# Preparing the first unit of gated linear attention inside the input projection

## The chip, the cores and the metric

One Trainium2 core runs one program. The time is device microseconds of one execution; smaller is better. Before the change three timed executions gave 2419.51, 2427.17 and 2428.51 us (median 2427.17).

## The reference, cut to what matters

Two transformer blocks run one after the other on 1024 tokens of width 1024. The part that the change touches is the first block's input projection and its gated linear attention (GLA):

```python
z = n @ w_in[i]
gq, gk, gv, g_low, g_r, c_q, c_kv, k_r = split_cols(z, IN_SPLITS)
...
log_a = jax.nn.log_sigmoid((g_low @ gla_gate_w2[i] + gla_gate_b[i]).astype(jnp.float32)) / GLA_TAU
...
b = jnp.cumsum(gi, axis=2)
o_inter = jnp.einsum('bhtk,bhkv->bhtv', qi * jnp.exp(b), state)
scores = jnp.einsum('bhtk,bhsk,bhtsk->bhts', qi, ki, decay)
...
o_g = rms_norm(o_g, gla_out_norm[i]).reshape(B, S, GLA_WIDTH) * jax.nn.silu(g_r)
```

The scores need query and key multiplied by decays that are made from the running sum `b` of the log gates. The second block's modulation, `silu(cond) @ ada_w + b`, is also computed inside the GLA program.

## The kernel before, in words

The kernel is a row of programs, each an `nc.Block()` with a hand-written instruction order for each engine and a barrier behind it. Two of them matter here.

**`project_and_prepare`** (tiles `pp_*`) multiplies the normed input by `w_in`, group of columns by group, and at the same time prepares the queries and keys of the softmax attention (MLA). Its time runs in steps `s`: each step is one projection slot on TensorE (24 matmuls of 256 columns in the last 32 slots), and from step 5 on each token tile `t` of 128 tokens takes a period of 7 steps (`piece(s)`), in which TensorE makes the up-projections (`queries_up`, `keys_up`) and, for the tile before, four groups of transposes `turn(t-1, m)`. Each turned group goes through one PSUM bank (`turn_bank`): ScalarE copies it out (`high`, L614), VectorE takes the remainder (`low`, L784), and only then may TensorE turn the next. ScalarE also takes each projected result out of its bank (`take`, L573; two banks, so the slot two further on waits for it), and VectorE normalises (`normed`) and rotates (`rope`) the heads. SyncE stores the results with DMAs, the last of them behind the last `low`.

**`gated_linear_attention`** (tiles `gla_*`) works on 4 units (token half by pair of heads) of 4 chunks each. A unit needs a preparation, `prep(u, 0..3)`: TensorE multiplies the gates (`gates`, L1386, a float32 matmul), ScalarE makes the logarithm (L1140 to L1143), VectorE the running sum (L1262) and the differences for each level (L1240), ScalarE the exponentials (L1154 to L1173), VectorE the five decayed queries `qs` (L1251) and GpSimd the five decayed keys `ks` (L1104). The preparation of unit u+1 is spread over the chunks of unit u. That of unit 0 has no cover: nothing can be scored before it (`scores(0)`, L1398 and L1405). After the scores of the next chunk come `outputs(n)` and, after every even chunk up to 10, `modulate` (L1460): 8 matmuls over two pieces `ada_w` of 1 MB that stream from HBM through 4 buffers. SyncE issues all loads in the order of its program.

## Time and profile before

| | |
|---|---|
| profiled execution, time | 2428.71 us |
| its span on the core | 2426.9 us |
| median of three timed executions | 2427.17 us |
| TensorE busy in the span | 2274.8 us (94%) |
| input projection, until the GLA program's first instruction | 0 to 273.7 us |
| GLA program | 273.7 to about 394 us |

The profile comes from one execution. Its time lies 1.8 us above its span, and 1.5 us above the median of the timed ones. A row of the timeline gives start, duration, engine, line, operation and, in brackets, how long the engine sat idle before it and what ended that. A releaser is inferred from semaphore events.

### The profile page before, as it was taken

To read this page: it belongs to the slowest core of one execution; us is meant where nothing else is said; L and a number is where in the kernel's file an instruction comes from. 1 tells how busy PE (TensorE), PEld (TensorE's weight loads), DVE (VectorE), ACT (ScalarE), POOL (GpSimd) and SP (SyncE) were. 2 spreads that over 40 slices of the span, in tenths; PEclk is the share of its full clock that TensorE was granted. 3 is DMA by queue.
4 is the path that set the end of the run, shared out by engine and by line. 5 is a ranking of instruction groups with operands and counts; after the bars stand their busy time and mean duration, and the time that the engine had idled before them with its cause. 6 is when DMAs were issued, how large, how long until landed. Compare 5 with 4: busy or idle time off the path is not lost. (4 is left out here: it accounts for less than half of the span.)

```text
span 2426.9 us, 31960 instructions
## 1 busy us (share of the span) xinstructions
PE 2274.8 (94%) x12292; PEld 1889.2 (78%) x12292; DVE 1126.7 (46%) x1992; ACT 976.5 (40%) x1993; POOL 861.4 (35%) x755
## 2 busy tenths in 40 slices
PE   6999487979999999999999999999999899999798
PEld 6799346967888888888887887888888688888566
DVE  4555486861522222222223535044421788888435
ACT  5434344861523113112113426233221677677422
POOL 5433153543323123123123216332210577777331
PEclk9999688999999999999999999999999899999999
DMA  5455745522111112012012112366656335533231
GB/s 149 104 159 132 226 166 166 135 67 74 46 54 57 33 50 70 25 50 66 29 46 65 57 35 66 113 177 204 188 149 179 100 92 128 142 96 96 100 126 78
DMA packets 202281, 248.48 MB, mean 102 GB/s; under 512 B 63592, under 2 KB 123384, under 8 KB 202128
## 3 DMA queue, kind: packets, MB, share of 16 engines
q1 hardware_dynamic: 196368, 240.14, 34.5%
q10 hardware_dynamic: 5760, 6.29, 0.8%
q8 instruction: 97, 1.59, 0.3%
q14 instruction: 56, 0.46, 0.1%
HBM read 172.88 MB, written 65.10 MB: 98 GB/s over the span
## 5 line engine op out<-in xcount | busy, mean ns | idle before, releaser
L2088 POOL TENSOR_TENSOR rm_w_lo<-rm_stage,rm_w_hi 128x512 fp32r<-128x512 f32 x192 | 246.8, 1298 | 653.8 <-ACT rm_w_hi L2158 653.2
L2158 ACT ACTIVATE rm_w_hi<-rm_stage 128x512 fp32r<-128x512 f32 x192 | 118.2, 628 | 287.8 <-PE rm_down L242 234.4
L2795 DVE TENSOR_REDUCE da_low_score<-da_scores 128x1 f32<-128x1280 f32 x128 | 190.3, 1488 | 31.2 <-PE da_scores L2675 31.1
L242 PE MATMUL rm_down<-rm_w_hi,rm_h_hi 128*128 128x512 f32 x512 | 203.7, 398 | 0.0
L242 PE MATMUL rm_down<-rm_w_lo,rm_h_hi 128*128 128x512 f32 x512 | 203.0, 396 | 0.0
L242 PE MATMUL rm_down<-rm_w_hi,rm_h_lo 128*128 128x512 f32 x512 | 202.9, 396 | 0.0
L2346 DVE TENSOR_TENSOR residual<-residual,rm_down 128x512 f32<-128x512 f32 x128 | 87.5, 687 | 225.8 <-PE rm_down L242 225.1
L2778 POOL TENSOR_TENSOR da_prob<-da_prob 128x1280 f32<-128x1280 f32 x64 | 188.2, 2941 | 5.3
L2736 ACT ACTIVATE da_prob<-da_scores,da_low_score 128x1280 f32<-128x1280 f32 x128 | 170.7, 1334 | 7.3 <-DVE da_low_score L2795 7.3
L2675 PE MATMUL da_scores<-da_k_hi,da_q 128*128 128x512 f32 (+1 forms) x384 | 151.7, 395 | 20.3 <-ACT da_prob L2736 9.2
L2337 DVE TENSOR_TENSOR rm_act_r<-rm_act_r 128x512 f32<-128x512 f32 x64 | 45.5, 711 | 222.2 <-ACT rm_act_r L2201 222.2
L2776 POOL TENSOR_SCALAR da_prob<-da_prob,da_ratio 128x1280 f32<-128x1280 f32 x64 | 86.0, 1343 | 173.4 <-DVE da_ratio L2803 173.2
L2675 PE MATMUL da_scores<-da_k_lo,da_q 128*128 128x512 f32 (+1 forms) x384 | 133.7, 364 | 0.0
L2745 ACT ACTIVATE da_aT_hi<-da_turn 128x512 fp32r<-128x512 f32 (+1 forms) x192 | 94.8, 532 | 62.9 <-PE da_turn L2689 62.7
L2810 DVE TENSOR_TENSOR da_aT_lo<-da_turn,da_aT_hi 128x512 fp32r<-128x512 f32 (+1 forms) x192 | 109.1, 596 | 22.1 <-ACT da_aT_hi L2745 20.3
L2201 ACT ACTIVATE rm_act_r<-rm_up 128x512 f32<-128x512 f32 x64 | 38.5, 601 | 194.0 <-PE rm_up L242 193.9
L242 PEld LDWEIGHTS rm_down<-rm_w_hi,rm_h_lo 128*128 128x128 f32 x512 | 96.5, 189 | 23.5
L242 PEld LDWEIGHTS rm_down<-rm_w_lo,rm_h_hi 128*128 128x128 f32 x512 | 96.6, 189 | 23.1
L242 PEld LDWEIGHTS rm_down<-rm_w_hi,rm_h_hi 128*128 128x128 f32 x512 | 96.6, 189 | 23.0
L242 PE MATMUL rm_up<-xa_hi,rm_w_hi 128*128 128x512 f32 x288 | 113.1, 393 | 0.7 <-POOL xb_lo L2116 0.7
L242 PE MATMUL rm_up<-xa_lo,rm_w_hi 128*128 128x512 f32 x288 | 112.7, 391 | 0.0
L242 PE MATMUL rm_up<-xb_hi,rm_w_hi 128*128 128x512 f32 x288 | 112.1, 389 | 0.5 <-POOL rm_w_lo L2088 0.5
(395 smaller groups left out, 6216.4 us busy)
## 6 DMA issues: line engine op xcount, KB each, us to landing
rm_stage<-in_w_mlp_up SPq DMA_DIRECT2D x64, 256.0 KB, 2.8
rm_stage<-in_w_mlp_down SPq DMA_DIRECT2D x64, 256.0 KB, 2.9
rm_stage<-in_da_w_in SPq DMA_DIRECT2D x64, 256.0 KB, 3.3
gla_ada_w<-in_ada_w SPq DMA_DIRECT2D x12, 1024.0 KB, 6.9
da_k_hi<-dk_hi SPq DMA_DIRECT2D x32, 320.0 KB, 7.5
da_k_lo<-dk_lo SPq DMA_DIRECT2D x32, 320.0 KB, 9.1
dp_swapped<-dp_x SPq DMA_DIRECT2D x128, 64.0 KB, 2.0
da_q<-dq SPq DMA_DIRECT2D x32, 256.0 KB, 6.1
```

The costliest lines, as they stand in the source:

```text
L242: last = nc.tensor.matmul(out, x, y, start=(n == 0), stop=(n == total - 1))
L2088: nc.gpsimd.tensor_tensor(lo, stage[:, n % SLOTS], hi.bitcast(F32), ALU.subtract).then_inc(w_lo_ready, 1)
L2158: nc.scalar.activation(hi, stage[:, n % SLOTS], ACT.Copy).then_inc(w_hi_ready, 1)
L2337: nc.vector.tensor_tensor(act_r[:, n % 2], act_r[:, n % 2], act_r[:, n % 2], ALU.mult)\
L2346: nc.vector.tensor_tensor(c.H[:, t, cols_of(half)], c.H[:, t, cols_of(half)], down_bank[n % 5][:], ALU.add).then_inc(down_added, 1)
L2675: last = nc.tensor.matmul(scores[z][:, at:end], q[s][:, z, qt * P:(qt + 1) * P], k[s][:, z, at:end], start=(i == 0), stop=(i == 1))
L2736: nc.scalar.activation(prob[:, n % BUF, z], scores[z][:, 0:K], ACT.Exp, scale=-1.0, bias=low_score[:, n, z:z + 1], accum_out=sums[:, n, z: ...
L2745: nc.scalar.activation(aT_hi[:, n // 2 % 2, j:e, (n % 2) * P:(n % 2 + 1) * P], turn_bank(i)[:, 0:(e - j) * P].rearrange("p (j q) -> p j q" ...
L2776: nc.gpsimd.tensor_scalar(p1, p1, ratio[:, n:n + 1], 1.0, ALU.mult, ALU.mult).then_inc(rest_scaled, 1)
L2778: nc.gpsimd.tensor_tensor(p0, p0, p1, ALU.add).then_inc(prob_ready, 1)
L2795: nc.vector.tensor_reduce(out=low_score[:, n, z:z + 1], in_=scores[z][:, 0:K], op=ALU.min, axis=AX.X).then_inc(low_score_ready, 1)
L2810: nc.vector.tensor_tensor(aT_lo[:, n // 2 % 2, j:e, q], turn_bank(i)[:, 0:(e - j) * P].rearrange("p (j q) -> p j q", q=P), aT_hi[:, n // 2 ...
```

## The change: what it does

The preparation of GLA's unit 0 moves into the last period of `project_and_prepare`. A class `GlaFirst` holds its tiles (`gf_*`) across both programs and issues its steps at fixed places: the gate columns are turned at steps 54 and 55, the gates multiplied at 56, query and key loaded back from HBM behind step 57, ScalarE's parts come at 57, 59, 61 and 63, VectorE's behind `normed(7)`, between `low(6, 2)` and `low(6, 3)`, and behind `rope(7, 1)`; GpSimd's five decayed keys come at its end. The tiles are laid over others: `gf_qk` is the weight stage, `gf_qs` and `gf_ks` lie over the up-projection's operands. The last tile's turned groups alternate between `turn_bank` and `up_bank[0]`. The projection's groups are ordered so that the output gate (which needs Silu) comes before the values. The gate columns no longer go to HBM and back (`zc`). In the GLA program the values and gates are loaded in three parts, and query, key, values and gate of the second half behind the third `ada_w` piece. SBUF tiles of later programs are placed anew ("combined layout"), the scratch for dynamic DMAs shrinks; neither adds or moves an instruction.

```diff
+class GlaFirst:
...
+        self.qk = sb("qk", [P, 2, 2, UT])
+        self.diff = sb("diff", [P, 2, UT])
...
+            self.cT = up_sb("cT_hi", [P, 2, 3, P]), up_sb("cT_lo", [P, 2, 3, P])
+            self.wq = up_sb("wq_hi", [P, 2, 768]), up_sb("wq_lo", [P, 2, 768])
+            self.wk = up_sb("wk_hi", [P, 1024]), up_sb("wk_lo", [P, 1024])
+        self.qs, self.ks = sb("qs", [P, NQ + 1, UT]), sb("ks", [P, NQ + 1, UT])
...
+    def turn_low(self, pe, half, bank, zc, ident):
+        if half:
+            pe.wait_ge(self.gl_ready, half)
+        for i in range(4):
+            last = self.nc.tensor.transpose(bank[0:GR, i * P:(i + 1) * P], zc[:, 4 * half + i, 0:GR], ident[:])
+        last.then_inc(self.gl_turned, 1)
...
+    def gates(self, pe, bank):
+        pe.wait_ge(self.gl_ready, 2)
+        pe.wait_ge(self.loaded, 32)
+        self.nc.tensor.matmul(bank[:], self.w2[:, 0:P], self.glowT[:, 0:self.UT], start=True, stop=True)\
+            .then_inc(self.pre_ready, 1)
...
+    def logarithm(self, act, bank):
+        act.wait_ge(self.pre_ready, 1)
+        self.nc.scalar.activation(self.mag[:], bank[:], ACT.Abs, bias=self.gb[:, 0:1]).then_inc(self.mag_ready, 1)
+        act.wait_ge(self.mag_ready, 1)
+        self.nc.scalar.activation(self.mag[:], self.mag[:], ACT.Exp, scale=-1.0).then_inc(self.act_done, 1)
+        act.wait_ge(self.act_done, 1)
+        self.nc.scalar.activation(self.mag[:], self.mag[:], ACT.Ln, bias=1.0).then_inc(self.ln_ready, 1)
...
+    def level(self, act, i):
+        act.wait_ge(self.diff_ready, i + 1)
+        if i == 2:
+            act.wait_ge(self.q_used, 1)
+            act.wait_ge(self.k_used, 1)
+        self.nc.scalar.activation(self.diff[:, i % 2], self.diff[:, i % 2], ACT.Abs).then_inc(self.act_done, 1)
+        act.wait_ge(self.act_done, 2 + i)
+        self.nc.scalar.activation(self.expo[:, i % 2], self.diff[:, i % 2], ACT.Exp, scale=-1.0 / self.TAU)\
+            .then_inc(self.exp_ready, 1)
...
+    def across(self, act):
+        act.wait_ge(self.q_used, 3)
+        act.wait_ge(self.k_used, 3)
+        self.nc.scalar.activation(self.expo[:, 0], self.b[:], ACT.Exp, scale=1.0 / self.TAU).then_inc(self.exp_ready, 1)
+        act.wait_ge(self.diff_ready, 5)
+        act.wait_ge(self.q_used, 4)
...
+    def running_sum(self, dve, bank):
+        nc = self.nc
+        dve.wait_ge(self.loaded, 32)
+        dve.wait_ge(self.mag_ready, 1)
+        nc.vector.tensor_scalar(self.low[:], bank[:], self.gb[:, 0:1], 0.0, ALU.add, ALU.min).then_inc(self.low_ready, 1)
+        dve.wait_ge(self.low_ready, 1)
+        dve.wait_ge(self.ln_ready, 1)
+        nc.vector.tensor_tensor(self.low[:], self.low[:], self.mag[:], ALU.subtract).then_inc(self.dve_done, 1)
+        dve.wait_ge(self.dve_done, 1)
+        dve.wait_ge(self.reset_ready, 2)
+        nc.vector.tensor_tensor_scan(self.b[:], self.reset[:], self.low[:], 0.0, ALU.mult, ALU.add).then_inc(self.b_ready, 1)
+        dve.wait_ge(self.b_ready, 1)
+        self.difference(0, 2 * self.LEVELS[0], self.LEVELS[0] - 1).then_inc(self.diff_ready, 1)
+        self.difference(1, 2 * self.LEVELS[1], self.LEVELS[1] - 1).then_inc(self.diff_ready, 1)
...
+    def upper_levels(self, dve):
+        self.decayed_query(dve, 0, 1, self.expo[:, 0])
+        self.difference(0, 2 * self.LEVELS[2], self.LEVELS[2] - 1).then_inc(self.diff_ready, 1)
+        self.decayed_query(dve, 1, 2, self.expo[:, 1])
+        self.difference(1, 16, 7).then_inc(self.dve_done, 1)
+        dve.wait_ge(self.dve_done, 2)
+        self.nc.vector.tensor_scalar(self.diff[:, 1], self.diff[:, 1], 80.0 * self.TAU, -80.0 * self.TAU, ALU.min, ALU.max)\
+            .then_inc(self.diff_ready, 1)
+
+    def lower_levels(self, dve):
+        self.decayed_query(dve, 2, 3, self.expo[:, 0])
+        self.difference(0, P, P - 1, -1).then_inc(self.diff_ready, 1)
+        self.decayed_query(dve, 3, 4, self.expo[:, 1])
+
+    def last_level(self, dve):
+        dve.wait_ge(self.exp_ready, 6)
+        self.nc.vector.tensor_copy(self.dec[:, 0], self.expo[:, 0].rearrange("p (c t) -> p c t", t=P)[:, :, P - 1])\
+            .then_inc(self.dve_done, 1)
+        self.decayed_query(dve, 4, 6, self.expo[:, 0])
...
-    first_col = [None, 0, GW, NCOL, NCOL + GW, g_r, g_r + GW]
+    first_col = [None, 0, GW, g_r, g_r + GW, NCOL, NCOL + GW]
+    GATE = (3, 4)
...
+    LOAD_FIRST = 57
+    LOW_TURNS, GATES = (54, 55), 56
+    LOGARITHM, UPPER, LOWER, ACROSS = 57, 59, 61, 63
...
+            return up_bank[0] if t == TT - 1 and m % 2 else turn_bank
...
-                    sp.wait_ge(copied, TT)
-                    sp.dma_start(d["zc"].rearrange("t p n -> p t n"), zc[:, :, 0:GR]).then_inc(z_stored, 16)
...
+                if s == LOAD_FIRST:
+                    sp.wait_ge(w_lo_ready, GROUPS * KT)
+                    for i in range(RING):
+                        n = max(m for m in range(first_out[1], first_out[3]) if m % RING == i)
+                        sp.wait_ge(stored[i], 16 * stores_at(n))
+                    for place, at in ((first.q, 0), (first.k, 2)):
+                        sp.dma_start(place, d["gqk"][at:at + 2, :, 0:NCOL].rearrange("k p s -> p k s"))\
+                            .then_inc(first.qk_loaded, 16)
...
+            pool.wait_ge(first.qk_loaded, 32)
+            pool.wait_ge(up_k_ready, TT)
+            first.decayed_key(pool, 0, 1, first.expo[:, 0])
+            first.decayed_key(pool, 1, 2, first.expo[:, 1])
+            first.decayed_key(pool, 2, 3, first.expo[:, 0])
+            first.decayed_key(pool, 3, 5, first.expn[:])
+            first.decayed_key(pool, 4, 7, first.expo[:, 1])
...
+                if s in LOW_TURNS:
+                    first.low_out(act, LOW_TURNS.index(s), c_bank)
+                if s == LOGARITHM:
+                    act.preload_act_table_set("natural_log_exp_and_others")
+                    act.wait_ge(first.loaded, 32)
+                    first.logarithm(act, c_bank)
+                if s == UPPER:
+                    act.wait_ge(up_k_ready, TT)
+                    first.level(act, 0)
+                    first.level(act, 1)
+                if s == LOWER:
+                    first.level(act, 2)
+                    first.both_signs(act)
+                if s == ACROSS:
+                    first.across(act)
...
+                if t == TT - 1:
+                    first.running_sum(dve, c_bank)
...
+                    first.upper_levels(dve)
...
+                    first.lower_levels(dve)
+                    first.last_level(dve)
...
+                read = 4 * t + m - (1 if t == TT - 1 and m else 0)
+                pe.wait_ge(*((lo_ready, read) if read else (x_lo_ready, 2 * TT)))
...
+                    if s == LOW_TURNS[0]:
+                        pe.wait_ge(c_lo, 3 * TT)
+                    first.turn_low(pe, LOW_TURNS.index(s), c_bank, zc, c.ident)
+                if s == GATES:
+                    first.gates(pe, c_bank)
...
+        parts = (slice(0, 1), slice(1, CH), slice(CH, TT))
...
+            def load_second():
+                sp.dma_start(q[1][:], d["gqk"][0:2, :, second].rearrange("k p s -> p k s")).then_inc(qk_loaded[1], 16)
+                sp.dma_start(k[1][:], d["gqk"][2:4, :, second].rearrange("k p s -> p k s")).then_inc(qk_loaded[1], 16)
+                load_tokens(v, "gv", 2, v_loaded)
+                load_tokens(gate, "gr", 2, gate_loaded)
...
+                if m == 2:
+                    load_second()
...
-            for i in range(CH):
-                prep(0, i)
...
-            gates(0)
+            scores(0)
             gates(1)
-            scores(0)
-            pe.wait_ge(v_loaded, 16)
```

What moves on ScalarE, in `project_and_prepare`, steps 57 to 60. Before (each `pp_ring` row is a `take`, each `pp_qk_hi` row a `high`):

```order
L614 ACTIVATE pp_qk_hi<-pp_turn 96x512 [waits pp_q_out,pp_turned]
L573 ACTIVATE pp_ring<-pp_ps 128x256 [waits pp_stored2,pp_result_ready]
...
L614 ACTIVATE pp_qk_hi<-pp_turn 96x512 [waits pp_q_out,pp_turned]
L573 ACTIVATE pp_ring<-pp_ps 128x256 [waits pp_stored3,pp_result_ready]
...
L573 ACTIVATE pp_ring<-pp_ps 128x256 [waits pp_stored0,pp_result_ready]
...
L614 ACTIVATE pp_qk_hi<-pp_turn 96x512 [waits pp_q_out,pp_turned]
```

After:

```order
L784 ACTIVATE pp_qk_hi<-pp_turn 96x512 [waits pp_q_out,pp_turned]
L845 ACT_TABLE_LOAD
L317 ACTIVATE gf_mag<-pp_turn,gf_gb 128x512 [waits gf_pre_ready,gf_loaded]
...
L321 ACTIVATE gf_mag<-gf_mag 128x512 [waits gf_act_done]
L743 ACTIVATE pp_ring<-pp_ps 128x256 [waits pp_stored2,pp_result_ready]
...
L784 ACTIVATE pp_qk_hi<-pp_turn 96x512 [waits pp_q_out,pp_turned]
L743 ACTIVATE pp_ring<-pp_ps 128x256 [waits pp_stored3,pp_result_ready]
...
L328 ACTIVATE gf_diff<-gf_diff 128x512 [waits gf_diff_ready,pp_up_k_ready]
L330 ACTIVATE gf_expo<-gf_diff 128x512 [waits gf_act_done]
...
L743 ACTIVATE pp_ring<-pp_ps 128x256 [waits pp_stored0,pp_result_ready]
...
L784 ACTIVATE pp_qk_hi<-pp_turn 96x512 [waits pp_q_out,pp_turned]
```

A table load and seven activations now stand among the takes and the copies; the first `gf_diff` waits for VectorE.

VectorE in the same program from the end of `normed(7)`, before:

```order
L757 TENSOR_TENSOR residual<-pp_up,pp_rsh 128x4x64
L754 TENSOR_TENSOR residual<-pp_up,pp_rsh 128x384
L757 TENSOR_TENSOR residual<-pp_up,pp_rsh 128x4x64
L761 TENSOR_TENSOR residual<-residual,pp_rsh 128x8x32
L784 TENSOR_TENSOR pp_qk_lo<-pp_turn,pp_qk_hi 96x512 [waits pp_hi_ready,pp_dve_step]
L784 TENSOR_TENSOR pp_qk_lo<-pp_turn,pp_qk_hi 96x512 [waits pp_hi_ready]
```

After (the `L970` rows are `low(6, 2)` and `low(6, 3)`; the rotation of tile 7 starts with the last row; 3 more of the queries and one difference stand behind the rotation, ahead of `low(7, 0)`):

```order
L947 TENSOR_TENSOR residual<-residual,pp_rsh 128x8x32
L362 TENSOR_SCALAR gf_low<-pp_turn,gf_gb 128x512 [waits gf_mag_ready,gf_loaded,pp_dve_step]
L365 TENSOR_TENSOR gf_low<-gf_low,gf_mag 128x512 [waits gf_ln_ready,gf_low_ready]
L368 SCALAR_TENSOR_TENSOR gf_b<-gf_reset,gf_low 128x512 [waits gf_reset_ready,gf_dve_done]
L294 TENSOR_TENSOR gf_diff<-gf_b 128x512 [waits gf_b_ready]
...
L970 TENSOR_TENSOR pp_qk_lo<-pp_turn,pp_qk_hi 96x512 [waits pp_hi_ready]
L352 TENSOR_TENSOR gf_qs<-gf_qk,gf_expo 128x512 [waits gf_exp_ready,pp_up_k_ready,gf_qk_loaded]
L294 TENSOR_TENSOR gf_diff<-gf_b 128x512
...
L294 TENSOR_TENSOR gf_diff<-gf_b 128x512
L379 TENSOR_SCALAR gf_diff<-gf_diff 128x512 [waits gf_dve_done]
L970 TENSOR_TENSOR pp_qk_lo<-pp_turn,pp_qk_hi 96x512 [waits pp_hi_ready]
L956 TENSOR_TENSOR residual<-residual,pp_gq 128x768 [waits pp_norm_read]
```

Ten of the preparation's instructions now stand ahead of the rotation.

SyncE's loads at the start of the GLA program, before:

```order
L1054 DMA gla_glow<-zc 128x8x16
L1054 DMA gla_w<-in_gla_gate_w 16x256
L1054 DMA gla_gb<-in_gla_gate_b 128x2x1
L1054 DMA gla_qT<-gqk 128x2x512
L1054 DMA gla_kT<-gqk 128x2x512
L1054 DMA gla_causal<-in_gla_causal 128x128
L1054 DMA residual<-gv 128x8x512
L1054 DMA gla_gain<-in_gla_out_norm 128x1
L1054 DMA residual<-gr 128x8x512
L1054 DMA gla_qT<-gqk 128x2x512
L1054 DMA gla_kT<-gqk 128x2x512
...
L1067 DMA gla_ada_w<-in_ada_w 128x4x512
```

After (causal mask, norm gain, the two conditioning vectors and `ada_b` are left out):

```order
L1243 DMA residual<-gv 128x512
...
L1243 DMA residual<-gr 128x512
L1243 DMA residual<-gv 128x3x512
L1243 DMA residual<-gr 128x3x512
...
L1270 DMA gla_ada_w<-in_ada_w 128x4x512
...
L1270 DMA gla_ada_w<-in_ada_w 128x4x512 x2
L1275 DMA gla_ada_b<-in_ada_b 2x512
L1256 DMA gla_q<-gqk 128x2x512
L1257 DMA gla_k<-gqk 128x2x512
L1243 DMA residual<-gv 128x4x512
L1243 DMA residual<-gr 128x4x512
L1270 DMA gla_ada_w<-in_ada_w 128x4x512
```

The first `ada_w` piece now has 2 MB of values and gate ahead of it in the queue instead of 6 MB; 3 MB for the second half stand between the third and the fourth piece.

## Rows read from the trace of the kernel before

**Rows 1.** Busy time by window, from GLA's start to its first scores: columns as in the first row.

```profile
core 0: us, PE busy (x) PEld busy (x) DVE busy (x) ACT busy (x) POOL busy (x), PEclk, DMA share, GB/s
273.70:299.30 25.60, 6.02 (x12) 1.93 (x13) 13.82 (x16) 12.50 (x20) 9.49 (x9) 0.50 0.91 293
```

**Rows 2.** Timeline of SyncE's queue and TensorE, around that stretch.

```profile
268.83 0.54 SPq L451 DMA_DIRECT2D mqk_lo<-pp_qk_lo  x1
273.75 0.38 SPq L1054 DMA_DIRECT2D gla_glow<-zc  x1
...
299.30 0.45 PE L1398 MATMUL gla_ps<-ident,gla_ks 128*128 128x128 f32 x1 [13.55 <-POOL gla_ks L1104]
299.68 1.56 PE L1405 MATMUL gla_ps<-gla_qs,gla_ks 64*128 64x128 f32 x44
```

**Rows 3.** Timeline of ScalarE and VectorE, the uncovered preparation.

```profile
282.08 0.69 ACT L1140 ACTIVATE gla_mag<-gla_ps,gla_gb 128x512 f32<-128x512 f32 x1 [2.16 <-PE gla_ps L1386]
286.91 0.63 ACT L1154 ACTIVATE gla_diff<-gla_diff 128x512 f32<-128x512 f32 x1 [2.81 <-DVE gla_diff L1240]
...
297.35 0.68 DVE L1251 TENSOR_TENSOR gla_qs<-gla_qT,gla_expo 128x512 f32<-128x512 f32 x1
```

**Rows 4.** Timeline of VectorE and ScalarE, the projection's last 25 us.

```profile
249.07 0.39 ACT L573 ACTIVATE pp_ring<-pp_ps 128x256 f32<-128x256 f32 x1 [2.49 <-PE pp_ps L876]
...
246.14 0.41 DVE L761 TENSOR_TENSOR residual<-residual,pp_rsh 128x256 f32<-128x256 f32 x1
250.21 0.69 DVE L784 TENSOR_TENSOR pp_qk_lo<-pp_turn,pp_qk_hi 96x512 fp32r<-96x512 f32 x1 [3.65 <-ACT pp_qk_hi L614]
...
258.49 0.28 DVE L779 TENSOR_TENSOR residual<-pp_rop 128x128 f32<-128x128 f32 x1
...
267.77 0.69 DVE L784 TENSOR_TENSOR pp_qk_lo<-pp_turn,pp_qk_hi 96x512 fp32r<-96x512 f32 x1 [1.87 <-ACT pp_qk_hi L614]
```

**Rows 5.** Timeline: a gates matmul, a table load.

```profile
317.72 1.12 PE L1386 MATMUL gla_ps<-gla_glowT,gla_w 16*128 16x512 f32 x2
...
298.93 1.28 ACT L1199 ACT_TABLE_LOAD   x1
```

**Rows 6.** Timeline of VectorE and GpSimd, the same operations at two places.

```profile
288.91 1.76 DVE L1240 TENSOR_TENSOR gla_diff<-gla_b 128x512 f32<-128x512 f32 x1
309.82 0.68 DVE L1240 TENSOR_TENSOR gla_diff<-gla_b 128x512 f32<-128x512 f32 x1
...
288.38 3.42 POOL L1104 TENSOR_TENSOR gla_ks<-gla_kT,gla_expo 128x512 f32<-128x512 f32 x2 [13.24 <-ACT gla_expo L1155]
306.85 2.50 POOL L1104 TENSOR_TENSOR gla_ks<-gla_kT,gla_expo 128x512 f32<-128x512 f32 x2 [7.69 <-ACT gla_expo L1155]
```

**Rows 7.** Busy time by window (columns as in rows 1).

```profile
80.40:85.00 4.60, 0.30 (x3) 0.05 (x1) 1.35 (x3) 4.50 (x16) 4.35 (x6) 0.83 0.00 1
85.00:90.00 5.00, 4.96 (x12) 3.92 (x13) 0.00 (x0) 0.52 (x2) 4.74 (x7) 0.50 0.94 213
278.00:294.00 16.00, 4.96 (x8) 1.23 (x6) 9.66 (x9) 6.70 (x11) 4.74 (x3) 0.50 1.03 376
294.00:297.00 3.00, 0.00 (x0) 0.00 (x0) 2.96 (x6) 2.30 (x5) 1.26 (x1) 0.50 0.77 87
...
307.00:320.00 13.00, 11.84 (x142) 5.50 (x142) 11.58 (x28) 6.90 (x15) 11.10 (x10) 0.94 0.51 161
```

**Rows 8.** DMA issues, 255 to 325 us: line, engine, times, KB each, us to landing.

```profile
gla_ada_w<-in_ada_w SPq DMA_DIRECT2D x7, 1024.0 KB, 7.0
```

**Rows 9.** Timeline of TensorE, GLA chunks 0 to 4.

```profile
306.90 2.79 PE L1460 MATMUL gla_ps<-gla_ada_w,gla_cond 128*32 128x512 f32 x16
309.88 1.03 PE L1405 MATMUL gla_ps<-gla_qs,gla_ks 64*128 64x128 f32 x44
...
315.86 1.92 PE L1460 MATMUL gla_ps<-gla_ada_w,gla_cond 128*32 128x512 f32 x16
...
320.41 0.33 PE L1398 MATMUL gla_ps<-ident,gla_ks 128*128 128x128 f32 x1 [1.57 <-DVE gla_qs L1251]
```

263 lines of the change are left out of this document (152 added, 111 removed).

## The prediction

> **What bounds the kernel now.** I read the page first: TensorE is busy for 94% of the span (table above), so what can be won lies where it waits, and the two programs that the change touches hold the largest such place at hand. The windows view shows it: from the GLA program's first instruction at 273.7 us to its first scores at 299.3 us TensorE is busy for 6.0 of 25.6 us, at a granted clock of 0.50, the 1.2 of its two levels of 1.2 and 2.4 GHz [rows 1]. The timeline names the end of the wait: the first transpose (L1398) comes after 13.55 us idle, released by GpSimd's last decayed key [rows 2]. This is the chain of unit 0's preparation: ScalarE's first Abs at 282.1, its first level at 286.9, VectorE's last decayed query until 298.0 [rows 3]. DMAs run beside it at 376 GB/s, from 278 to 294 us [rows 7]: what the GLA program reads at its start is loaded under the same cover. In the projection ScalarE's takes wait for TensorE (2.49 us before the one at 249.07), which is bound by its own matmuls up to 258 us; behind it come the last four turned groups, through one bank each in turn, the last remainder starting at 267.77 [rows 4], then the last store, issued at 268.83, and the barrier, past at 273.75 [rows 2].
>
> **The change, step by step.** The sum is made against the profiled execution (span 2426.9 us, time 2428.7 us, 1.5 us above the median of the runs shown).
>
> 1. *Removed from the path.* Scores can start with the program, some 0.3 us in: 25.6 - 0.3 = 25.3 us.
>
> 2. *TensorE, steps 54 to 56.* A gates multiplication costs 1.12 us at full clock [rows 5]; the eight small transposes I take at 0.6 us together (an estimate: half of the gates). TensorE is the bound there, so the schedule behind moves by 1.7 us.
>
> 3. *ScalarE and VectorE, steps 57 to 61.* The table load (1.28 us [rows 5]) and three activations (from Abs to the next wait 2.0 us, at 0.63 to 0.69 each [rows 3]) go before the take of step 58, late by 1.0 us; `normed(7)`, which ended at 246.55 [rows 4], ends at about 249.2. The running sum and the first difference take as long as from Abs to level 0 less the wait for Abs, about 3.5 us [rows 3], so ScalarE, which has reached `level(0)` at 248.3 (the take of step 59 lies one slot of 2.9 us ahead of the one at 249.07, and 1.7 us are added), stands until 252.7. Behind it in its queue are the take of step 60 (249.07 before [rows 4]) and `high(6, 2)`; two levels are four activations at 0.63, so the take comes at 255.1 and the copy ends at 256.2. `low(6, 2)` follows (before: 250.21), then TensorE may turn `(6, 3)`, at 256.9: it stands for about 3 us, and ScalarE's takes of steps 61 to 63 are late by as much.
>
> 4. *VectorE until the end.* Behind `low(6, 2)` come five operations of the upper levels (four at 0.68 [rows 6], one at 0.43: 3.1 us), the second `low` (0.7), the rotation (before until 258.77 [rows 4], 4.7 us after `low(6, 3)`), then three queries, one difference and one copy, with ScalarE's two activations between: 4 us. That gives 265.2 for the rotation; GpSimd's third and fourth key (1.25 us each [rows 6]) fall into it. An uncovered difference took 1.76 us beside GpSimd and 0.68 us alone, GpSimd's pair 3.42 against 2.50 us [rows 6]; I take 1.5 us for both. The exponentials of `across` end at 269.3, the first copy of tile 7 at 269.9.
>
> 5. *The turned groups of tile 7.* With two banks they no longer take 2.55 us each. Two are done at 271.6, the other two are turned at half clock, and the last remainder ends at about 274.6 instead of 268.46. From there the store and barrier as before, 5.3 us, and 0.1 for the store just ahead: the GLA program starts at about 280.0, 6.3 us later. Bounds: 3 us (GpSimd never in the way, the waits overlap) and 11 us (the preparation's 16 us of chain [rows 3] not interleaved at all, with every GpSimd operation on VectorE's path).
>
> 6. *The cover of the loads is gone.* This is the second large term. Ahead of `modulate(0)` lie now 2.2 MB of values, gate and mask and two 1 MB pieces; ahead of the second half of `modulate(1)` 9.5 MB in all (2.2, three pieces, 3.1 for the second half, a piece). Flow starts some 2 us after the program. The big loads flow at 376 GB/s, and near 294 us the stream dips to 87 GB/s for 3 us, where the conditioning vectors are fetched as single elements [rows 7]. I charge 1 us of the 3 (an estimate: the two vectors are 8 KB, and the queue ahead of them is shorter now). The second piece is there at 2 + 1 + 4.3/0.376 = 14.4 us after the start. Scores, gates, scores and outputs at half clock would bring TensorE to `modulate` at 9.1 us; so it ends at 15.8 (four of its eight matmuls, half of 2.79 us [rows 9], behind the piece): 295.8 instead of 309.7. VectorE and ScalarE are no faster: unit 1's logarithm, done ahead of the first scores before, and the Silu of the conditioning vectors with two table loads (1.28 us each) now stand behind the first keys; by the same durations ScalarE squares chunk 0 at 14 us, 13.7 us earlier than before, the value that I take. With the same distance `modulate(1)` would start at 302.2 (before 315.86 [rows 9]), 22.2 us after the start, but its fourth piece is there only at 2 + 1 + 9.5/0.376 = 28.3. It ends at 29.3, 309.3 instead of 317.8: 8.5 us earlier. Bounds: no stall (rival A), or 2 us more, if the dip keeps its whole 3 us. The scores of chunk 4 had waited 1.57 us for VectorE [rows 9], which the stall covers: 310.8 instead of 320.4.
>
> Behind this nothing is removed or added; the later pieces find buffers freed one `modulate` earlier, as before. The remaining edits cost nothing: the gate columns' store and its reload (no TensorE wait hangs on SyncE at 85 us), the memset of `reset` (GpSimd idles then), the order of groups (the one Silu table load falls into a slot with over 2 us of slack on ScalarE); were that cover gone, it is 1.3 us. The new layout moves no instruction.
>
> **Sum:** 25.3 - 6.3 (later start) - 9.4 (loads, with what VectorE's wait gives back) = 9.6 us: a span of 2417.3, a time of 2419.1 us in a profiled execution, 2417.6 in the median.
>
> On the rate of the loads the Trainium skill (DMA: Bandwidth & Descriptors, Where 436 GB/s comes from) has another number: for HBM to SBUF about 358 GB/s binds. By that rule the fourth piece comes 1.2 us later and the gain is 8.4 us; the 16 us window of [rows 7] is above it, so the trace decides.
>
> **Rivals.**
>
> *A: the second load is not in the way* (22%). If the queue's pieces land as early as in the trace, 7.0 us behind their issue [rows 8], `modulate(1)` doesn't wait, and the limit is ScalarE's 13.7 us, to which VectorE's wait of 1.57 us may add. Against: those pieces were issued into a queue that had run dry [rows 7]. Gain 13.7 to 15.3 us: 2412.5.
>
> *B: the tail grows more* (18%). VectorE and GpSimd collide on more than two of the five keys, or TensorE's 3 us stall drops its clock (0.30 us busy in 4.6 us, then a clock of 0.50 from 85 to 90 us [rows 7]), so that the last two projection slots take 5 instead of 3 us. Price 1.1 us for each collision [rows 6] and 4 us for the clock, 5 to 7 in all: gain 2 to 5 us, 2423.5. For the collisions the Trainium skill has the rule (SBUF — State Buffer, Who interferes with whom): a VectorE instruction with two SBUF inputs contends with a GpSimd instruction that reads SBUF, and the later one blocks until the other is through. By it, three more blocked operations cost up to 1.25 us each, 3.8 us, and the time would be 2421.4; [rows 6] agree, with 1.08 us for one.
>
> *C: slower, by the clock* (5%). In GLA TensorE's granted clock is 0.50 up to the first scores and 0.94 from 307 to 320 us [rows 1, 7]. Scores cost 1.56 us at the one and 1.03 at the other, `modulate` 2.79 and 1.92 [rows 2, 9]; a chunk, in which scores are one of four such groups of products, costs some 2 us more at half clock (an estimate). The stalls in both `modulate` thin out TensorE's work just where the clock had risen. From five more chunks at half clock on the gain is gone; if all twelve that ran faster fall back, with `modulate` 28 us are lost: 2446.
>
> *D: it doesn't do what it says* (5%). Something in the first chunk (mask, first values, the table loads and the Silu of the conditioning vector now behind `keys(0)`) takes the place of the removed wait wholly: within 3 us of before, 2427.
>
> The forecast holds 50%.
>
> **How the numbers follow.** Half a per cent is 12.1 us, about what a measurement of this kernel can tell from no change. Faster by more: all of A (22%) and a quarter of the forecast's half (12%), which reaches from 6 to 13.7 us: 34%. Slower: C and a point of D and B: 6%. The rest, 60%, within. The three runs of before lie 9 us apart, which widens the range at both ends: 2409 (A with a us or two) to 2426 (B's end); left out are 4% below and C, most of D and some of B above, 14%. The forecast alone: 2413 to 2421.
>
> **What would show it.** Right: the first scores within 1 us of the program's start; ScalarE idle before the first `gf_diff` at about 248 to 252.7; TensorE idle about 3 us before a turned group at 257; the barrier at 280 +- 1.5; `modulate(0)` idle until about 15 us and `modulate(1)` until 28 us after the start, released by DMA; scores of chunk 4 at 311. Wrong: no wait for a DMA in `modulate(1)` (A), a barrier behind 284 (B), a clock at 0.50 beyond chunk 4 (C), scores that start 20 us after the barrier (D). I would be most wrong where the two waits, in the tail and at the loads, are counted one after the other while the second only takes up what the first left.

## The result and the profile after

Five runs of the changed kernel took 2407.03 to 2414.78 us, median 2410.21; five of the kernel before 2419.51 to 2428.51, median 2422.97. The ratio is 0.9942, 95% interval 0.9924 to 0.9961: 0.6% or some 13 us faster (9 to 18), where 9.6 us were forecast, with 60% on a change within half a per cent. The profiled execution of the changed kernel took 2407.03 us (span 2405.2, granted clock 0.974), that of before 2428.7 (2426.9, 0.968). The two profiles are 21.7 us apart: before was profiled in one of its slowest executions, after in its fastest, so the profiles alone would tell too large an effect.

The timeline of the changed kernel, from unit 0's levels in the projection to the scores of chunk 4 (start, duration, engine; in brackets the idle time before and what ended it):

```profile
251.36 0.63 ACT L328 ACTIVATE gf_diff<-gf_diff 128x512 f32<-128x512 f32 x1 [4.82 <-DVE gf_diff L294]
...
255.46 1.06 PE L1113 MATMUL pp_turn<-ident,residual 128*96 128x128 f32 x4 [3.34 <-DVE pp_qk_lo L970]
...
268.59 0.69 DVE L970 TENSOR_TENSOR pp_qk_lo<-pp_turn,pp_qk_hi 96x512 fp32r<-96x512 f32 x1 [0.57 <-ACT pp_qk_hi L784]
...
272.00 0.69 DVE L970 TENSOR_TENSOR pp_qk_lo<-pp_up,pp_qk_hi 96x512 fp32r<-96x512 f32 x1 [0.17 <-ACT pp_qk_hi L784]
...
273.06 0.62 SPq L604 DMA_DIRECT2D mqk_lo<-pp_qk_lo  x1
...
278.60 0.35 SPq L1243 DMA_DIRECT2D residual<-gv  x1
...
278.79 0.45 PE L1580 MATMUL gla_ps<-ident,gf_ks 128*128 128x128 f32 x1 [7.45 <-PEq L432]
...
290.43 0.22 ACT L1396 ACTIVATE gla_cond<-gla_cond_in 128x16 f32<-128x16 f32 x1 [4.36 <-DMA gla_cond_in<-in_c_ctx]
...
294.68 1.93 PE L1645 MATMUL gla_ps<-gla_ada_w,gla_cond 128*32 128x512 f32 x8 [7.20 <-DMA gla_ada_w<-in_ada_w]
...
297.29 1.93 PE L1645 MATMUL gla_ps<-gla_ada_w,gla_cond 128*32 128x512 f32 x8 [0.69 <-DMA gla_ada_w<-in_ada_w]
...
299.16 0.48 PE L1580 MATMUL gla_ps<-ident,gf_ks 128*128 128x128 f32 x1
...
311.92 1.06 PE L1645 MATMUL gla_ps<-gla_ada_w,gla_cond 128*32 128x512 f32 x8 [3.76 <-DMA gla_ada_w<-in_ada_w]
...
314.41 0.48 PE L1580 MATMUL gla_ps<-ident,gla_ks 128*128 128x128 f32 x1
```

Against [rows 2] the first scores are at 278.79 and not at 299.30, 0.2 us behind the program's first load, and the 13.55 us wait for GpSimd is gone. The price in the projection is there too: ScalarE stands 4.82 us at level 0, TensorE 3.34 us ahead of a turned group, and the GLA program begins at 278.60 instead of 273.75. Then four rows show new waits, all for DMA: ScalarE's Silu stands 4.36 us for the conditioning vectors, TensorE 7.20 and 0.69 us for the modulation's first two pieces and 3.76 us for the fourth. Chunk 4, at 320.41 in [rows 9], comes at 314.41: of 20.5 us won at the first scores 6.0 are left after four chunks.

The windows of the same stretch (busy time of each engine, granted clock, DMA share, GB/s) say why:

```profile
255.40:258.70 3.30, 3.24 (x16) 3.24 (x17) 3.27 (x7) 2.12 (x4) 0.29 (x1) 0.51 0.03 8
278.60:299.20 20.60, 12.53 (x117) 5.83 (x117) 9.59 (x18) 9.14 (x14) 4.85 (x6) 0.50 0.84 262
278.00:282.00 4.00, 3.21 (x47) 1.79 (x47) 0.63 (x3) 1.56 (x2) 0.78 (x2) 0.50 0.52 141
282.00:286.00 4.00, 4.00 (x50) 2.48 (x50) 1.87 (x4) 3.16 (x4) 0.00 (x0) 0.50 0.86 274
286.00:290.00 4.00, 1.47 (x6) 1.09 (x4) 3.12 (x7) 0.07 (x1) 0.00 (x0) 0.50 0.67 131
290.00:294.00 4.00, 0.00 (x0) 0.00 (x0) 0.00 (x0) 3.48 (x7) 0.44 (x1) 0.50 0.92 296
294.00:318.00 24.00, 18.88 (x189) 7.33 (x189) 12.28 (x30) 8.62 (x18) 11.93 (x11) 0.71 1.05 386
```

The first window is the one behind TensorE's 3.34 us wait in the projection: its granted clock is 0.51 there. From the GLA program's start TensorE is busy for 12.5 of 20.6 us where it was for 6.0 of 25.6 [rows 1], still at 0.50. The DMA engines run at 386 GB/s from 294 to 318 us, so the queue is the bound there; but in the four windows ahead they moved only 141, 274, 131 and 296 GB/s, and what is missing there (2.8 MB against the full rate) comes later. An `ada_w` piece now lands 9.5 us behind its issue (7.0 in [rows 8]):

```profile
gla_ada_w<-in_ada_w SPq DMA_DIRECT2D x9, 1024.0 KB, 9.5
```

The time of every stage, from the start of its first TensorE instruction in the timeline, for sixteen profiles (us; "to latent" is from the first scores to the start of the latent program (the softmax attention behind GLA, tiles `ma_*`), "down" from the first up-projection of the MLP in `residual_to_differential` (tiles `rm_*`: the output projection, the MLP and the next block's input projection) to the first scores of the differential attention (`da_*`), "differential" from there to the last program's first sum):

| kernel profiled | first scores | to latent | latent starts | down | differential |
|---|---|---|---|---|---|
| before, before_again, before_pad32 | 299.3, 299.1, 299.0 | 97.2, 97.2, 98.3 | 396.5, 396.3, 397.2 | 1242.2, 1243.3, 1243.1 | 400.9, 400.0, 397.7 |
| before_pad224, layout_only | 299.0, 298.8 | 97.2, 97.1 | 396.2, 395.9 | 1232.3, 1232.1 | 399.6, 395.7 |
| changed, after_pad256, after_pad512 | 278.8, 277.6, 276.8 | 112.9, 113.3, 113.2 | 391.7, 390.9, 390.0 | 1232.1, 1232.8, 1231.8 | 394.5, 396.9, 400.8 |
| after_pad32, after_pad128 | 278.8, 280.2 | 113.9, 113.9 | 392.7, 394.1 | 1241.9, 1240.4 | 398.4, 400.1 |
| single_bank | 280.3 | 113.0 | 393.3 | 1232.0 | 398.0 |
| second_half_later, cond_early | 279.1, 278.9 | 109.7, 111.5 | 388.8, 390.4 | 1231.7, 1233.4 | 399.4, 397.2 |
| weights_first, weights_first_cond | 279.5, 278.9 | 114.2, 111.2 | 393.7, 390.0 | 1232.0, 1231.7 | 401.3, 395.9 |
| all_loads | 276.5 | 99.7 | 376.2 | 1232.0 | 399.4 |

Of the 21.7 us between the two profiles 4.8 are there when the latent program starts, which gives 1.7 back; 10.1 come in "down" (see the column), 6.4 in "differential" and 1.9 in the last program. The "down" column has two groups, 1231.7 to 1233.4 and 1240.4 to 1243.3, by kernel and not by execution. "Differential" ranges from 394.5 to 401.3 us in no order of kernels, so I take it for spread between executions, and with it most of the last 8 us.

### The profile page after: what moved, and what is told of

Same layout as the page of the kernel before. It is cut to its first block and busy times, and to the rows that moved or that the text cites. A ratio compares the mean times of both kernels' runs of the same rounds, so it can differ in the third digit from the quotient of the medians.

```text
span 2405.2 us, 31974 instructions
## 1 busy us (share of the span) xinstructions
PE 2256.6 (94%) x12292; PEld 1881.4 (78%) x12292; DVE 1123.9 (47%) x1992; ACT 973.9 (40%) x1994; POOL 862.1 (36%) x755
## 5 line engine op out<-in xcount | busy, mean ns | idle before, releaser
L244 PE MATMUL rm_up<-xa_hi,rm_w_lo 128*128 128x512 f32 x288 | 112.1, 389 | 0.0
```

What stands on the lines that cost most here:

```text
L244: last = nc.tensor.matmul(out, x, y, start=(n == 0), stop=(n == total - 1))
```

## Experiments: where does the rest come from?

**The layout alone.** Theory: the traces differ by 10 us in a stage whose instructions the change doesn't touch, so the new places of the tiles do it. Rival: the executions differ.

```
-    c.H = c.sb("residual", [P, TT, D])
+    c.H = c.sb("residual", [P, TT, D], side="right")
...
+    ..., dynamic_dma_scratch_size=1024)
```

before_again is before unchanged; layout_only is before with every hunk of the change that sets a tile's place (residual, differential attention, `rm_*`, last program, DMA scratch) and no other.

> The kernel before, unchanged, profiled a second time. The profiled execution of before was one of its slower ones (2428.7 us, with its runs from 2419.5 to 2428.5), so some of the 21.7 us between the two profiles may be spread between executions and not the change. If the spread sits in one stage (the waits at half clock in the two programs around the change, say), that stage moves between the two profiles of before and the others stay within 0.5 us; if the down projection of the residual network, which took 233 ns a matmul in before and 227 in the changed kernel, is a property of the kernel and not of the execution, it reads 233 again. Ratio 1.00, span 2418 to 2427.

> The kernel before with the whole of the combined layout (residual at the other end of SBUF, the small DMA scratch, the new places of the differential attention's, the residual network's and the last program's tiles) and none of the first unit's move. My prediction gave the layout nothing: by it the time stays at before's, 0 +- 1 us. The rival, read from the two traces: the down projection's matmuls follow each other at 227 ns instead of 233 (1536 of them, 10 us), the differential attention saves 4 to 6 us more: 12 to 17 us faster, so that the move of the unit itself is worth next to nothing or even costs time.

The second profile of before agrees with the first within 0.4 us at the latent start and within 1.2 us in "down"; its ratio is 1.0006 (0.9995 to 1.0018). layout_only, median 2412.20, has 0.9945 (0.9934 to 0.9957): 13 us faster, as much as the whole change. All of "down" is in it, nothing of the GLA program. The lines by form (count, busy, mean ns of one) for 700 to 1200 us, before and then changed:

```profile
L242 PE MATMUL rm_down<-rm_w_hi,rm_h_hi 128*128 128x512 f32 x368 | 145.5, 395 | 0.0
L242 PE MATMUL rm_up<-xa_hi,rm_w_hi 128*128 128x512 f32 x180 | 70.0, 389 | 0.0
```

```profile
L244 PE MATMUL rm_down<-rm_w_hi,rm_h_hi 128*128 128x512 f32 x363 | 141.2, 389 | 0.0
...
L244 PE MATMUL rm_up<-xa_hi,rm_w_hi 128*128 128x512 f32 x188 | 73.1, 389 | 0.0
```

The up-projection keeps its 389 ns; the down-projection, the same shape, reads 395 before and 389 after. These durations overlap; the distance of two starts in the timeline is 233.3 against 226.7 ns, and 1536 such matmuls (8 groups, 8 token tiles, 2 halves, 4 chunks, 3 products) make 10.1 us.

**Which place?** `rm_h` is the stationary operand there. In before it starts at byte 196,032 of a partition, in the changed kernel at 67,744.

```
         with ExitStack() as early:
+            c.sb("rm_pad", [P, 8], ctx=early)
             h_hi, h_lo = (c.sb(f"rm_h_{x}", [P, FT, S], F32R, ctx=early) for x in ("hi", "lo"))
```

The 8 words are 32 bytes; the other kernels of this group have 32, 56, 64 and 128 in its place (128, 224, 256 and 512 bytes).

> The kernel before with 32 bytes in front of the two hidden tiles rm_h, and nothing else moved: they start at 196,064 and 212,448 bytes of a partition in place of 196,032 and 212,416. If it is the start address within 64 bytes (0 in before, 32 in the changed kernel, 32 for all other tiles that the residual network's matmuls load) that costs 6.7 ns a matmul, the down projection falls to 227 ns and the kernel is 10 us faster. If it is the upper end of the partition (above about 196,000 bytes), or something else, it stays at 233 ns and within 1 us of before.

> The changed kernel with the same 32 bytes in front of rm_h: they start at 67,776 and 84,160, both multiples of 64, low in the partition. If the start address within 64 bytes decides, the down projection goes up to 233 ns a matmul and the kernel is 10 us slower than the changed one (2420). If the upper end of the partition decides, it stays at 227 ns and 2410.

before_pad32 stays at 233.3 ns (ratio 1.0003), which speaks against the start address within 64 bytes; after_pad32 goes up to 233.3 (0.9987, 0.9976 to 0.9998), which speaks against the upper end of the partition. Both theories fell. What I tried next was the distance from the start of `rm_w`, the moving operand, to that of `rm_h`: 288 and 320 bytes over a multiple of 512 in before and before_pad32, 32 in after_pad32, 0 where it is fast.

> The kernel before with 224 bytes in front of rm_h and nothing else moved, so that rm_h starts at 196,256: its distance to the weights rm_w_hi (124,064) is then a multiple of 512 bytes, as in the changed kernel and in all pairs that ran at 227 ns, while in before (288 over a multiple), before_pad32 (320) and after_pad32 (32) it isn't. If the distance of the two operands decides, rm_h's matmuls fall from 233.3 to 226.7 ns and this one line gives 10 us, most of what layout_only gave (12). If the upper end of the partition is what costs in before (and something else in after_pad32), they stay at 233.3 and the time at before's.

> The changed kernel with 512 bytes in front of rm_h (distance to the weights a multiple of 512 still, no longer of 1024 or 2048). If multiples of 512 are what counts, 226.7 ns a matmul and no loss; if it is 1024 or 2048, 233.3 ns and 10 us lost.

> The changed kernel with 256 bytes in front of rm_h (distance 256 over a multiple of 512). If every multiple of 64, 128 or 256 bytes does, 226.7 ns; if it has to be 512, as the theory so far has it, 233.3 ns and 10 us lost.

> The changed kernel with 128 bytes in front of rm_h (distance to the weights 128 over a multiple of 256). Multiples of 256 bytes ran at 226.7 ns so far (0, 256, 512), distances of 32, 64 (in the projection), 288 and 320 at 233. If it has to be a multiple of 256, 233.3 ns and 10 us lost; if 128 will do, 226.7 and no loss.

Lines of before_pad224 and of after_pad32, the same view:

```profile
L242 PE MATMUL rm_down<-rm_w_hi,rm_h_hi 128*128 128x512 f32 x366 | 142.4, 389 | 0.0
```

```profile
L244 PE MATMUL rm_down<-rm_w_hi,rm_h_hi 128*128 128x512 f32 x364 | 143.9, 395 | 0.0
```

| kernel | `rm_h_hi` at | the same, modulo 256 | start less that of `rm_w_hi`, modulo 256 | ns from start to start |
|---|---|---|---|---|
| before | 196,032 | 192 | 32 | 233.3 |
| before_pad32 | 196,064 | 224 | 64 | 233.3 |
| before_pad224 | 196,256 | 160 | 0 | 226.7 |
| changed, layout_only | 67,744 | 160 | 0 | 226.8, 226.7 |
| after_pad32 | 67,776 | 192 | 32 | 233.3 |
| after_pad128 | 67,872 | 32 | 128 | 232.5 |
| after_pad256 | 68,000 | 160 | 0 | 226.8 |
| after_pad512 | 68,256 | 160 | 0 | 226.8 |

What the pads show: the place of `rm_h` modulo 256 bytes sets the rate. Shifts by 256 and 512 bytes leave it (so 512, as I had put it, isn't needed), shifts by 32 and 128 cost 6.5 and 5.7 ns, and 224 bytes in front of it in before take 6.6 ns away. What they don't show is that the distance to `rm_w` is what counts. `rm_w_hi` starts 160 bytes over a multiple of 256 in all these kernels (124,064 and 114,848), so the third and the fourth column move together, and `rm_h`'s own start fits as well as the distance. No kernel moved `rm_w` and left `rm_h`. One other pair of this program speaks against the distance alone: `rm_pT` (stationary, at 196,032 in before and 67,744 in the changed kernel) with `rm_proj` (moving), 16,384 bytes apart in both kernels. In before its matmuls follow each other at 229.8 ns, in the changed kernel at 227.2. The lines of `--tile rm_proj_hi` (shortest, median and longest duration in ns), before and then changed:

```profile
L242 PE MATMUL rm_down<-rm_proj_hi,rm_pT_hi x32: 389/397/478, 1381.9 to 1477.8; 128*128 128x512 f32 x32
```

```profile
L244 PE MATMUL rm_down<-rm_proj_hi,rm_pT_hi x32: 389/389/476, 1369.1 to 1464.5; 128*128 128x512 f32 x32
```

before_pad224, one line, is at ratio 0.9973 (0.9961 to 0.9985), 6.6 us (4 to 9); its profile has the whole 10 us in "down" (the table), and I can't say where the difference of 3 us lies. after_pad32 is at the same time a measurement of the unit's move (and the rest of the layout) with the slow matmuls left in: 0.9987, 3 us (0.5 to 6).

**The loads behind the removed cover (step 6).** The changed kernel with its queue in another order, one edit at a time and together:

```
-                if m == 2:
+                if m == 3:
                     load_second()
+                if m == 5:
+                    load_second_values()
```

is second_half_later (`load_second` keeps queries and keys, the new function takes values and gates). In cond_early the two loads of `cond_in` stand behind that of `first.gb`, in the projection. weights_first moves the loads of chunks 1 to 3 (and the small one of the norm gain behind them) from ahead of the loop over the pieces into it:

```
-            load_tokens(v, "gv", 1, v_loaded)
-            load_tokens(gate, "gr", 1, gate_loaded)
...
+                if m == 1:
+                    load_tokens(v, "gv", 1, v_loaded)
+                    load_tokens(gate, "gr", 1, gate_loaded)
```

weights_first_cond has the last two edits, all_loads all three.

> The changed kernel with the loads of the second half put behind the modulation's weights that are needed first: queries and keys behind piece 3 in place of piece 2, values and gates behind piece 5. Step 6 of my prediction puts the second of the two new waits on these 3 MB: TensorE's 3.8 us wait for ada_w inside modulate(1) at 308 to 312 goes, the scores of chunk 4 come at 310.6 in place of 314.4, and if nothing behind takes it up, the latent program starts 3.8 us earlier (388 in place of 391.7). The rival: what follows (VectorE and ScalarE bound every chunk, or the second half's queries now come late for chunk 4) takes it up, and the latent program starts within 1 us of 391.7.

> The changed kernel with the two loads of the conditioning vectors (64 bytes a partition, in 4-byte pieces) moved from the GLA program's queue to the middle of the projection. In the changed kernel they hold the queue from 281.5 to 286.4 us, DMA moves 131 GB/s at 286 to 290 us, and ScalarE's Silu waits 4.36 us for them at 286.1 to 290.4, with unit 1's levels behind it. If step 6 was too small because of these loads, piece 1 of ada_w lands 3 to 4 us earlier, modulate(0) ends at 295 to 296 us in place of 299.2, and the latent program starts 3 to 4 us earlier (about 387.5, against 388.9 to 391.7 in four profiles of the changed kernel's GLA program). If the loads' bytes alone set it, the pieces come less than 1 us earlier.

> The changed kernel with the conditioning vectors early, the modulation's first two pieces ahead of chunk 1's values and gates, and the second half's loads behind pieces 3 and 5. By the theory that step 6's waits are the queue's order and not the work, modulate(0) starts at 287 to 288 us in place of 294.7, the scores of chunk 4 come at 305 to 308 in place of 312 to 314.4, the latent program starts at 383 to 385 us, and the time is 4 to 8 us below the changed kernel's. The rival: the granted clock falls in the new place or the engines behind bound the chunks, and the time stays within 2 us of second_half_later's (4 us below the changed kernel's).

> The changed kernel with one edit of all_loads alone: the modulation's first two pieces ahead of chunk 1's values and gates. From the first scores to the latent program's start: 97.2 us in the kernels with before's unit, 113.4 (112.9 to 113.9) in five profiles of the changed kernel's GLA program, 109.7 with second_half_later's edit, 111.5 with cond_early's, 99.7 with all three. If the order of these 1.5 MB carries most, it is 103 to 105 us here and the time some 8 us under the changed kernel's; if the three only work together (the Silu still waits for the conditioning vectors until start + 12, and modulate(1) for the second half), it stays above 109.

> weights_first together with cond_early's edit, so that of all_loads only the later place of the second half's loads is missing (109.7 against 113.4 us by itself, 3.7). If the edits add, the stretch is 3 to 4 us above all_loads's: 103.5 us; if the second half's 3 MB no longer stand in the way once the queue starts earlier, 100 to 101 us; if the first two together are what misses, 109 and more.

TensorE in second_half_later: modulate(1), at 308.16, waits for nothing.

```profile
294.80 1.93 PE L1649 MATMUL gla_ps<-gla_ada_w,gla_cond 128*32 128x512 f32 x8 [7.01 <-DMA gla_ada_w<-in_ada_w]
...
308.16 1.92 PE L1649 MATMUL gla_ps<-gla_ada_w,gla_cond 128*32 128x512 f32 x16
...
312.78 0.33 PE L1584 MATMUL gla_ps<-ident,gla_ks 128*128 128x128 f32 x1 [1.64 <-DVE gla_qs L1444]
```

In cond_early modulate(0) begins at 292.57, 2.1 us earlier than in the changed kernel (3 to 4 were expected), and TensorE still waits 3.70 us in modulate(1).

In weights_first the wait has moved: 0.90 and 2.99 us at modulate(0), but 8.65 at modulate(1). One piece takes TensorE 1.06 us at 288.68, at full clock, and 1.94 us behind the long wait, at half clock.

```profile
288.68 1.06 PE L1646 MATMUL gla_ps<-gla_ada_w,gla_cond 128*32 128x512 f32 x8 [0.90 <-DMA gla_ada_w<-in_ada_w]
...
292.73 1.07 PE L1646 MATMUL gla_ps<-gla_ada_w,gla_cond 128*32 128x512 f32 x8 [2.99 <-DMA gla_ada_w<-in_ada_w]
...
311.14 1.94 PE L1646 MATMUL gla_ps<-gla_ada_w,gla_cond 128*32 128x512 f32 x8 [8.65 <-DMA gla_ada_w<-in_ada_w]
```

In all_loads 0.15, 1.31 and 0.96 us are left, and chunk 4 comes at 300.25, ScalarE's Silu without a wait at 283.80:

```profile
276.50 0.45 PE L1587 MATMUL gla_ps<-ident,gf_ks 128*128 128x128 f32 x1 [7.30 <-PEq L434]
...
283.80 0.22 ACT L1403 ACTIVATE gla_cond<-gf_cond_in 128x16 f32<-128x16 f32 x1
...
285.34 1.31 PE L1652 MATMUL gla_ps<-gla_ada_w,gla_cond 128*32 128x512 f32 x8 [0.15 <-DMA gla_ada_w<-in_ada_w]
...
287.96 1.06 PE L1652 MATMUL gla_ps<-gla_ada_w,gla_cond 128*32 128x512 f32 x8 [1.31 <-DMA gla_ada_w<-in_ada_w]
...
297.59 1.07 PE L1652 MATMUL gla_ps<-gla_ada_w,gla_cond 128*32 128x512 f32 x8 [0.96 <-DMA gla_ada_w<-in_ada_w]
...
300.25 0.33 PE L1587 MATMUL gla_ps<-ident,gla_ks 128*128 128x128 f32 x1 [0.54 <-DVE gla_qs L1447]
```

```profile
276.30:300.20 23.90, 20.53 (x242) 10.66 (x242) 16.81 (x38) 14.88 (x26) 12.13 (x12) 0.80 0.96 340
280.00:284.00 4.00, 4.00 (x50) 2.77 (x50) 2.13 (x3) 3.44 (x5) 0.00 (x0) 0.50 0.95 318
288.00:292.00 4.00, 4.00 (x59) 1.88 (x60) 3.70 (x6) 2.26 (x5) 3.02 (x4) 1.00 1.06 383
```

| kernel | median us (before beside it) | ratio to before, interval | first scores to latent |
|---|---|---|---|
| changed | 2410.21 (2422.97) | 0.9942, 0.9924 to 0.9961 | 112.9 |
| second_half_later | 2406.22 (2421.28) | 0.9929, 0.9910 to 0.9949 | 109.7 |
| cond_early | 2407.34 (2420.74) | 0.9944, 0.9927 to 0.9960 | 111.5 |
| weights_first | 2406.10 (2425.15) | 0.9931, 0.9909 to 0.9954 | 114.2 |
| weights_first_cond | 2406.56 (2425.15) | 0.9928, 0.9906 to 0.9949 | 111.2 |
| all_loads | 2394.18 (2420.74) | 0.9886, 0.9867 to 0.9904 | 99.7 |

Taken singly the edits give 3.7, 1.9 and -0.8 us of the stretch of 113.4 (mean of the five profiles with the changed kernel's queue, which lie within 1.0 us), the pair of weights_first_cond 2.2; all three give 13.7. In the times only all_loads stands apart from the changed kernel; the intervals of the other four overlap with its own. The other two pairs of edits weren't run. They don't add, because the same bytes stand ahead of modulate(1)'s second half until the second half's 3.1 MB go behind it: bring modulate(0) forward and TensorE waits the longer at modulate(1); clear only modulate(1) and modulate(0) still waits 7 us. For weights_first this is the second of the two outcomes that I had written down (above 109, if the edits only work together), and for weights_first_cond the third (109 and more). The expectation for all_loads was too modest: 376.2 for the latent start and not 383 to 385, 14 to 16 us below the changed kernel and not 4 to 8. With no long wait left the clock is granted: 0.80 over 276.3 to 300.2 us, 1.00 from 288 to 292 us, where the changed kernel had 0.50 until 299.2. How much of the 13.7 us is the waits themselves and how much the clock, I haven't separated. all_loads is the fastest version, 1.1% under before, and beats both kernels.

**The second bank in the tail (step 5).**

```
-            return up_bank[0] if t == TT - 1 and m % 2 else turn_bank
+            return turn_bank
-                read = 4 * t + m - (1 if t == TT - 1 and m else 0)
+                read = 4 * t + m
```

> The changed kernel with the last token tile's turned groups through one bank, as in before, in place of two in turn (all four wait for the remainder ahead of them). Step 5 of my prediction took the tail with two banks at 274.6 us for the last remainder's end; measured 272.7. If the second bank is worth what the one-bank chain in before shows (a copy and a remainder per group one after another, 1.87 us of wait each), the last remainder ends 1.5 to 2.5 us later and the GLA program starts at 280 to 281; if the copies and rotations bound the tail anyway, it moves by less than 0.5 us.

VectorE's four remainders of tile 7 in that kernel, two of them:

```profile
266.50 0.69 DVE L970 TENSOR_TENSOR pp_qk_lo<-pp_turn,pp_qk_hi 96x512 fp32r<-96x512 f32 x1 [0.57 <-ACT pp_qk_hi L784]
...
274.17 0.69 DVE L970 TENSOR_TENSOR pp_qk_lo<-pp_turn,pp_qk_hi 96x512 fp32r<-96x512 f32 x1 [1.87 <-ACT pp_qk_hi L784]
```

They follow every 2.56 us, with the 1.87 us wait of [rows 4] ahead of the last three. From the start of the first to the end of the last there are 8.36 us, as in before (260.10 to 268.46), against 4.10 in the changed kernel (268.59 to 272.69): the second bank is worth 4.3 us there. The ends alone (274.86 against 272.69, 2.2 us) tell too little, because this execution was early: one and the same take of ScalarE near step 54 began at 227.41 here and at 228.90 in the changed kernel. after_pad512, where it began at 227.55, has its first scores at 276.8 against 280.3 here, 3.5 us, more than the 1.5 to 2.5 expected. One run, 2410.04 us, shows nothing of that in the time, and could not: it is inside the spread.

## Why the prediction was off, by its steps

- **Step 1** (25.3 us removed): held. The first scores come 0.2 us behind the program's first load, 0.3 was said.
- **Step 2** (1.7 us on TensorE): held, 2.0 us measured. From the turned group of step 54 to that of step 57 there are 14.53 us in the changed kernel (225.00 to 239.53) and 12.53 in before (226.84 to 239.37). The projection was 1.8 us early in this execution at step 54 already, which hides the cost in the absolute times.
- **Step 3**: held in kind. ScalarE stood 4.82 us at `level(0)` (4.4 said), TensorE 3.34 us for `low(6, 2)` (3 said), all of it 1.4 us earlier than written. What rival B had said of the clock came too: behind this wait it is 0.51 from 255.4 to 258.7 us, and twelve matmuls take 2.7 us (256.17 to 258.87) and not 1.4. That is 1.3 us and not the 4 that B charged, and the tail behind it ran over VectorE.
- **Step 4**: held. The rotation ended at 265.5 (266.7 said), with two operations of 1.28 and 1.40 us beside GpSimd.
- **Step 5** (last remainder 274.6, start 280.0, 6.3 us): measured 272.7, 278.6 and 4.85 us; in five profiles of the same code the first scores lay at 276.8 to 280.2, 20.6 us ahead of before's on average where steps 1 and 5 gave 19.0.
- **Step 6** (9.4 us given back, and "nothing is removed or added" behind): mechanism right, size wrong. Given back until the latent start: 16.0 us (113.4, the mean of five profiles with the changed kernel's queue, against 97.4, the mean of five with before's unit). `modulate(0)`'s second piece came at 18.7 us after the start and not 14.4, `modulate(1)`'s at 33.3 and not 28.3. So chunk 4 came 35.6 us after the first scores, 14.5 more than before, and 1 to 2 us more were lost behind it. What I mis-sized is the head of the queue: I charged 2 us for the start and 1 us for the conditioning vectors; the four windows from 278 to 294 us show 141, 274, 131 and 296 GB/s against 386 behind them, (245 + 112 + 255 + 90) x 4 us = 2.8 MB less, or 7.3 us. That is 4.3 us more than the 3 charged, as much as the second piece was late. SyncE's issue of the second vector's load alone took 4.07 us (282.25 to 286.32), so that the first `ada_w` load was issued at 286.37. cond_early takes the vectors away and wins 1.9 us of the stretch.
- **The layout** ("moves no instruction", costed at nothing): this is the step that failed. It moves no instruction, but changes the rate of 1536 of them, from 233.3 to 226.7 ns: 10 us in the traces, more than the unit's whole net.

The unit's move by itself: 20.6 - 16.0 = 4.6 us at the latent start (about half of the 9.6), 3 us (0.5 to 6) in after_pad32's runs. 10 us from the layout and 3 to 5 from the move make the 13 us measured. The times alone don't fix this division: layout_only is as fast as the changed kernel (0.9945 and 0.9942, 1 us apart), before_pad224 has 6.6 us for the 10 of its trace, and each ratio is good to 3 to 5 us. That the total of 13 us lies near the forecast 9.6 is luck: the move gave half of the forecast, and a term that I had put at nothing gave the rest.

Rival A (no wait at the second load) is refuted by the 3.76 us row; rival B (a barrier behind 284, 10 us later) by the 4.85 us; rival C by the time, and by the granted clock from chunk 4 to the latent start, 0.90 (before: 0.87); rival D (within 3 us of before) by the traces' 4.6 us alone, since the 13 us contain the layout's 10 and after_pad32's 3 us leave it close. The sentence on what would make it most wrong named the waits in the tail and at the loads, the second taking up what the first left. What the experiments show is the same thing between the two waits at the loads: in weights_first the wait goes from modulate(0) to modulate(1). Between the tail and the loads no run shows it.

On the rate of the loads, the window of 294 to 318 us has 386 GB/s, so the trace's rate was the right one to take. The Trainium skill's 358 GB/s (DMA: Bandwidth & Descriptors, Where 436 GB/s comes from) is below what this window shows.

## What to carry to other kernels

A wait that you remove was covering something: list the loads that ran under it in the queue's order, and reorder the queue by first use with the same change; here, against layout_only (0.9945), the move was worth 1 us with the old order of the loads (0.9942) and 14 with the new one (0.9886); at the latent start of the traces it is 4.6 and 20 us. Such loads shift their wait rather than lose it, so try the edits together: alone three of them gave 3.7, 1.9 and nothing, together 13.7 us of the stretch. When tiles move, compare the start-to-start times of equal matmuls in stages that the change doesn't touch before believing that a layout is free.
